# One accumulator bank and one ScalarE copy for the sample outputs of the RWKV-7 heads

## The reference, cut to what matters

```python
def step(S, inp):
    r_t, w_t, k_t, v_t, a_t, b_t = inp
    sa = jnp.einsum('bhvk,bhk->bhv', S, a_t)
    S = S * w_t[:, :, None, :] + sa[..., None] * b_t[:, :, None, :] + v_t[..., None] * k_t[:, :, None, :]
    return S, jnp.einsum('bhvk,bhk->bhv', S, r_t)
...
bonus = jnp.sum(rh * kh * W['rw_rk'][e].astype(f32), axis=-1, keepdims=True) * vh
ya = (head_norm(y, W['rw_ln'][e], A_LN_EPS) + bonus.reshape(Bsz, T, A_W)) * g.astype(f32)
```

## Time and profile before

| | before |
|---|---|
| median of three runs | 2313.78 us (2312.76 to 2318.72) |
| profiled execution | 2319.36 us, its span 2317.6 us |
| busy: PE, DVE, ACT, POOL | 2069.7, 1099.0, 690.4, 80.6 us |
| mean granted TensorE clock | 0.914 |

### The profile page before, as it was taken

How to read it: one execution, slowest core, us unless ns; L and a number is a source line. 1 busy time by engine, 2 the same in 40 slices (tenths; PEclk the granted TensorE clock), 3 DMA queues, 4 the chain that set the end, 5 groups by cost and what they waited for, 6 DMA issues and landing times.

```text
span 2317.6 us, 36907 instructions
## 1 busy us (share of the span) xinstructions
PE 2069.7 (89%) x15010; PEld 1876.9 (81%) x15010; DVE 1099.0 (47%) x1631; ACT 690.4 (30%) x963; POOL 80.6 (3%) x90
## 2 busy tenths in 40 slices
PE   8998666967667989999989998999899899999989
PEld 8996556856335779999989996666699889999988
DVE  5662776665463064234335764444563254234234
ACT  3323222222121143223224213322442243223222
POOL 0000110110000100000010000000000100000000
PEclk9998778977655989999999999889899999999999
DMA  5230000002001312222221322443332212222231
GB/s 197 85 99 5 1 0 0 0 0 95 19 1 46 122 61 91 91 91 91 91 100 55 127 91 109 165 172 145 118 112 93 87 55 91 91 91 91 91 100 55
DMA packets 44718, 186.70 MB, mean 81 GB/s; under 512 B 5480, under 2 KB 5992, under 8 KB 39272
## 3 DMA queue, kind: packets, MB, share of 16 engines
q1 hardware_dynamic: 44648, 185.72, 23.3%
HBM read 160.54 MB, written 25.16 MB: 80 GB/s over the span
## 4 chain that ended last, share of the span: by engine, by line
PE 76%; DVE 13%; DMA 4%; ACT 4%; issue 3%; POOL 0%; DVEq 0%; POOLq 0%; SPq 0%; ACTq 0%
PE ps L1965 52%; PE ps L1848 4%; PE ps L726 4%; PE ps L327 3%; DMA h_a<-in_rst 2%; DMA out_rst_o<-h_a 2%; DVE h_a L1735 2%; PE ps L1923 1%; ACT h_a L1794 1%; DVE free L409 1%; PE ps L345 1%; PE ps L1539 1%; PE ps L1522 1%; PE ps L1336 1%; DVE rb L364 1%
## 5 line engine op out<-in xcount | busy, mean ns | idle before, releaser
L1953 DVE TENSOR_TENSOR w_low<-slot,w_high 128x1024 fp32r<-128x1024 f32 x240 | 294.1, 1226 | 500.5 <-ACT w_high L1949 500.5
L1949 ACT ACTIVATE w_high<-slot 128x1024 fp32r<-128x1024 f32 x240 | 254.0, 1060 | 799.8 <-PE ps L1965 769.6
L1965 PE MATMUL ps<-x_high,w_high 128*128 128x260 f32 x1824 | 367.9, 283 | 1.1 <-issue 1.1
L1965 PE MATMUL ps<-x_high,w_low 128*128 128x260 f32 x1824 | 367.6, 283 | 0.0
L1965 PE MATMUL ps<-x_low,w_high 128*128 128x260 f32 x1824 | 367.0, 283 | 0.0
L1965 PE MATMUL ps<-hidden_high,w_low 128*128 128x260 f32 x1536 | 309.5, 283 | 0.0
L1965 PE MATMUL ps<-hidden_high,w_high 128*128 128x260 f32 x1536 | 309.4, 283 | 0.0
L1965 PE MATMUL ps<-hidden_low,w_high 128*128 128x260 f32 x1536 | 309.0, 283 | 0.0
L1965 PEld LDWEIGHTS ps<-x_high,w_high 128*128 128x128 f32 x1824 | 281.7, 189 | 1.8 <-issue 1.5
L1965 PEld LDWEIGHTS ps<-x_high,w_low 128*128 128x128 f32 x1824 | 281.2, 188 | 0.0
L1965 PEld LDWEIGHTS ps<-x_low,w_high 128*128 128x128 f32 x1824 | 280.4, 188 | 0.0
(11 more groups left out here) (588 smaller groups left out, 2608.2 us busy)
## 6 DMA issues: line engine op xcount, KB each, us to landing
slot<-in_w SPq DMA_DIRECT2D x240, 512.0 KB, 3.7
h_a<-in_rst SPq DMA_DIRECT2D x16, 1024.0 KB, 4.9
out_rst_o<-h_a SPq DMA_DIRECT2D x16, 1024.0 KB, 3.9
slot<-in_w SPq DMA_DIRECT2D x2, 2048.0 KB, 10.9
con<-in_con SPq DMA_DIRECT2D x1, 2126.0 KB, 16.5
h_a<-in_x SPq DMA_DIRECT2D x4, 520.0 KB, 5.1
h_a<-in_x SPq DMA_DIRECT2D x1, 2080.0 KB, 12.5
out_y<-h_a SPq DMA_DIRECT2D x8, 260.0 KB
```

What stands on the lines that cost most here:

```text
L1949: nc.scalar.activation(wh[c % 2], raw[c % 4], ACT.Copy).then_inc(s_wh, 1)
L1953: nc.vector.tensor_tensor(wl[c % 2], raw[c % 4], wh[c % 2].bitcast(F32), ALU.subtract).then_inc(s_wl, 1)
L1965: mm = pe.matmul(ps[:, 2 * par + hf, 0:HALF], w[c % 2][:, at], y(kt, hf), start=(start and kt == 0 and w is wh and y is x), stop=(stop and ...
```

## The change

The second heads' results go to bank 6 as well, onto rows 64 to 127 of the same 32 columns, and one copy over all 128 rows takes the place of the two over 64.

```diff
@@ act_rwkv1
             after(sp2, "y")
-            a.activation(xy[0:64], ps[0:64, 6, 0:32].rearrange("p (j t) -> p j t", j=4), ACT.Copy)
-            a.activation(xy[64:P], ps[64:P, 7, 0:32].rearrange("p (j t) -> p j t", j=4),
-                         ACT.Copy).then_inc(*sa.step("y"))
+            a.activation(xy, ps[:, 6, 0:32].rearrange("p (j t) -> p j t", j=4), ACT.Copy).then_inc(*sa.step("y"))
             yield
@@ pe_rwkv1
                         r = slice(64 * par, 64 * par + 64)
-                        mm = pe.matmul(ps[r, 6 + par, NS * j + b:NS * j + b + 1], sst[r, j, b, :],
+                        mm = pe.matmul(ps[r, 6, NS * j + b:NS * j + b + 1], sst[r, j, b, :],
                                        ua[r, j, TP + 1 + b:TP + 2 + b], start=True, stop=True)
             mm.then_inc(*sp2.step("y"))
```

## The result

| | before | after |
|---|---|---|
| median (lowest to highest) | 2313.27 us, 4 runs (2310.55 to 2318.72) | 2320.58 us, 4 runs (2319.82 to 2324.14) |
| ratio after/before | | 1.0029, 95% interval 1.0016 to 1.0043 |
| profiled execution | 2319.36 us, span 2317.6 us | 2319.82 us, span 2318.0 us |

The first measurement has the changed kernel 7.3 us slower. That is the other way than forecast and 0.6 us above the stated range. Repeated, the same two programs gave ratios from 0.9997 to 1.0023, with no order between them; the 7.3 us did not come back (experiments e0, e1, f1 to f4).

What follows compares the result with a forecast made beforehand. The prediction took TensorE to bound the kernel (busy 89% of the span), with the changed copies on the path in the first layer's mixer. Median 2313.78 us less 0.20 for the copy, plus 0.00 for the bank, gave 2313.6 us, range 2310.5 to 2320.

Steps and rivals of the forecast that it cites:

- the place on the path: The two ScalarE copies in the first layer's mixer lie on the path; the 0.20 us saved should reach the end whole.
- The price of the single copy: ScalarE, after the readout: one 128x32 copy takes 0.20 us, freeing ScalarE after 0.22 us instead of 0.42, saving 0.20.
- The mean matmul: L1044, consumer of the copies: starts 0.20 us sooner, worth nothing, as its result waits for VectorE until 642.80.
- Bank 6 for both heads: Readout matmuls, L1040: both row tiles writing one bank cost nothing; upper bound 25.6 us more.
- R1: Readout: the row tiles stop overlapping when both write bank 6; 6.3 us (2.4 to 9.2) more, 2319.9 us; chance 0.06.
- R2: Readout, L1040: each matmul waits for the previous one's end; 20.1 to 25.6 us more, 2333.7 to 2339.2 us; chance 0.04.
- The sum: Whole kernel: 0.20 us saved by the copy, 0.00 for the bank; 2313.6 us from the median of 2313.78.
- The range: Whole kernel: 2310.5 to 2320 us for 8 in 10 of all cases; chance 0.90 of staying within 0.3%.
- R3: ScalarE copy: costs 0.25 us or more, or something else holds L1146; gain 0 to 0.15 us, 2313.7 us; chance 0.04.
- R4: Later TensorE stretches in the mixer reach the upper clock level; L1336 alone 6.8 us less, 2306.8 us; chance 0.02.

Runs made afterwards that it cites:

- e0: The kernel before, unchanged, timed against itself: 2322.45 us, ratio 1.0023 (1.0009 to 1.0036).
- e1: The changed kernel, unedited, timed again against the kernel before: 2317.16 us, ratio 0.9997 (0.9980 to 1.0015).
- f1 to f4: Four unedited copies, in order the kernel before, changed, before, changed, against the kernel before: ratios 1.0005, 1.0002, 0.9999, 1.0011.
- e4: The kernel before with 32 more pairs of half-height copies (banks 6 and 7) ahead of the real pair: 2330.46 us, ratio 1.0056.
- e8: The kernel before with 64 more half-height copies, all of rows 0 to 63 of bank 6: 2322.81 us, one run.
- e9: The kernel before with 32 more pairs of half-height copies, both halves and all readout matmuls in bank 6: 2334.27 us, one run.
- e6: The kernel before with the 64 readout matmuls issued 16 times over into banks 6 and 7: 2422.51 us, ratio 1.0460.
- e7: The changed kernel with the 64 readout matmuls issued 16 times over, all into bank 6: 2427.44 us, ratio 1.0481 to the kernel before.
- e5: The changed kernel with 32 more 128-row copies of bank 6 ahead of the real one: 2319.32 us, ratio 1.0014 to the kernel before.

## Why the prediction was right or wrong

**What bounds, and the place on the path: right.** e4 shows it with 13 us in the trace and 13 us in the time. That the saving "should therefore reach the end of the kernel whole" holds as far as the third chunk with the late rise of the clock. At the mixer's end it came out as anything from 0.46 us to nothing, by execution.

**The price of the single copy: right in its duration, mis-sized in what it frees.** The copy lasts 0.197 us, as L989 did. The step that failed is "With the gap of 0.02 us that stands between the starts and ends above, ScalarE is free for L1146 after 0.22 us": I took the gap between half-height copies for a property of ScalarE's queue. It belongs to changes of rows (e4, e8, e9). The next instruction starts 0.093 us after the copy starts. The term was 0.20 us and measured 0.33 us. The rows of before had held no pair of waitless full-height instructions at this place, but the range "between 0.15 and 0.21" had no ground as an upper bound.

**The mean matmul: right.** L1042 starts sooner, and its result still waits for the reciprocal: VectorE takes it 3.27 us after the reciprocal starts, with two copies as with one.

**Bank 6 for both heads: right, at nothing.** Both R1 and R2 are refuted by 2048 records (e6, e7). In R2, the figure of 0.091 us per record is worked out with the 6.9 us of the 0.3% in it, so it is where the loss would pass 0.3%; the sign would turn at (4.6 + 0.2)/128 = 0.038 us. Nothing hangs on it. The sentence of the Trainium skill, "TensorEngine Tiling (Array Packing)", Restrictions and Gotchas, that different row tiles cannot access one bank simultaneously, costs no time here where the two tiles write different rows; the pace in one bank is that of two. The line that the Trainium skill, "PSUM — Partial Sum Buffer", PSUM bank collisions, draws by quadrants of a bank and its statement that nothing stalls agree with that pace.

**The sum: 0.33 us saved where 0.20 was forecast, both under what a time can show.** The mechanism was right and the size was off by 0.13 us.

**The range, and the direction: wrong.** The step that failed is "with the scatter of the runs before (1.0 below and 4.9 above their median) and about as much for another median below, so 2310.5 to 2318.5". Three runs around 2313.8 us stood for the kernel. Of 87 runs of the kernel before, the mean is 2318.2 us and the extremes are 2310.55 and 2326.61 us, 0.7% apart. The median I started from was itself some 4.4 us low, and "same as before" should have been centred near 2318 us with 4 us to either side. A sign was at hand: the profiled execution stood 5.58 us above the median, and I only noted it. The first ratio, 1.0029 with an interval that excludes 1, fits the same account. The changed kernel's 2320.58 us was ordinary, 0.8 us above the mean of its 36 later runs (2319.8); it was the four runs of before, with 2313.27, that lay low, 4.9 us under the mean of the 87. Why they did is not shown. By the standard deviation of 4.2 us, an estimate, the mean of four runs is as far off as theirs (2313.95) about once in twenty times, and theory D stays open. The interval is no guard against it; e0 has as narrow a one, 1.0009 to 1.0036, for no change at all.

**R3 (nothing measurable): so it is by the times, though not by its mechanism,** as the trace has the gain. **R4 (a gain through the clock)** saw a right source of differences, but not one that the edit steers: the pattern in the mixer moves single executions by about 3 us, unchanged copies show both patterns, and the profiles part ahead of the first changed instruction.

## What to carry to other kernels

Read the clock's pattern, not only its mean, before giving a range: where a kernel has stretches in which TensorE goes between its two levels, as this one has, a handful of runs may not fix its median, and the honest test for a change of under 0.3% is the same program against itself in the same session. For an edit this small the trace answers where the time cannot: multiply the touched instructions by 16 or 32, and both the pace and the path become measurable. On ScalarE, keep successive small instructions on the same rows where possible; alternating halves cost the overlap here, 0.20 us from start to start in place of 0.08. And a saving on a path through such stretches is best read at several points behind it, and compared between executions with the same clock pattern.

## What the runs showed of the hardware that I had not expected

- Two successive ScalarE copies of 32 columns from the accumulator start 0.08 us apart if they use the same rows (e5, e8), though each lasts 0.18 us or more. If the second uses other rows it starts only 0.01 to 0.03 us after the first has ended (e4, e8, e9), from one bank or from two.
- Row tiles of 64 rows that write different halves of one bank keep the pace of two banks: 1692 records in 90 us at the half clock in both cases (e6, e7), and 128 records within 3.70 us at the full clock (e0 with two banks, e1 with one).
- TensorE's clock changed level at different instructions in different executions of one program, in a stretch where the engine had the same work. Over the mixer four profiles of the kernel before fell into two groups, 152.3 and 152.6 us against 155.4 and 155.4 us.
